# ScalarE scales the softmax rows, sums are kept in PSUM, four weight units get their own buffers, the last tile is finished in column halves

## The reference, cut to what matters

```python
branches = jnp.einsum('bsnc,ncd->bsnd', ys, w_branch)
gates = jax.nn.sigmoid(g.reshape(bn, s_len, N_BRANCH, D_MODEL).astype(jnp.float32))
merged = jnp.sum(gates * branches, axis=2)
return merged @ w_out
...
h = layer_norm(DEEPNORM_ALPHA * h + mix, ln1_g[l], ln1_b[l])
ffn = peer_ffn(h, peer_wq[l], peer_subkeys[l], peer_u[l], peer_v[l])
h = layer_norm(DEEPNORM_ALPHA * h + ffn, ln2_g[l], ln2_b[l])
```

## Time and profile before

| | |
|---|---|
| median of 3 runs | 1730.18 us (1727.88 to 1731.35) |
| the profiled execution | 1732.18 us, span 1730.4 us |
| granted TensorE clock, mean | 0.995 of full speed |
| PE busy | 1689.1 us (98%) |
| DVE, ACT, POOL busy | 1255.8, 768.7, 820.7 us |

### The profile page before, as it was taken

One profiled execution on the slowest core, in us unless ns is written; L12 is line 12 of the kernel. 1 busy time (PEld: TensorE's weight loads), 2 busy tenths in 40 slices (PEclk: granted clock), 3 DMA queues, 4 the chain that ended last, 5 costly groups with the idle time before them and its releaser, 6 DMA issues.

```text
span 1730.4 us, 24570 instructions
## 1 busy us (share of the span) xinstructions
PE 1689.1 (98%) x9061; PEld 1486.3 (86%) x9061; DVE 1255.8 (73%) x2490; ACT 768.7 (44%) x1301; POOL 820.7 (47%) x496
## 2 busy tenths in 40 slices
PE   7999999999999999999999999999999999999997
PEld 6667767778878999999999999999888888888886
DVE  2487896562353778789888987534888888888886
ACT  4444444522232443775577367534333333333332
POOL 5222222344446466766777677776433232332312
PEclk9999999999999999999999999999999999999998
DMA  5111111224233365899799789997999999999952
GB/s 200 61 62 50 59 60 54 77 94 146 84 112 110 113 197 186 306 372 345 253 333 384 249 286 386 383 364 296 405 390 354 384 376 351 383 372 354 389 190 85
DMA packets 126360, 417.65 MB, mean 241 GB/s; under 512 B 12961, under 2 KB 32417, under 8 KB 124705
## 3 DMA queue, kind: packets, MB, share of 16 engines
q1 hardware_dynamic: 70176, 232.81, 38.2%
q0 software_dynamic: 36864, 134.23, 20.6%
q10 hardware_dynamic: 19200, 49.03, 7.2%
HBM read 364.91 MB, written 50.86 MB: 240 GB/s over the span
## 4 chain that ended last, share of the span: by engine, by line
PE 88%; DVE 8%; ACT 2%; issue 1%; DMA 1%; POOL 0%; SPq 0%; another core or an unknown queue 0%; ACTq 0%; DVEq 0%; POOLq 0%
PE ps L1285 16%; PE ps L1287 16%; PE ps L1286 16%; PE ps L1514 11%; PE ps L1511 11%; PE ps L1512 11%; PE ps L1609 5%; PE ps L1370 1%; DVE dist_a L842 1%; DVE row L895 1%; DVE row L866 1%; DVE small L841 1%; PE ps L1395 1%; DVE small L892 1%; DMA raw<-w_units 0%
## 5 line engine op out<-in xcount | busy, mean ns | idle before, releaser
L1285 PE MATMUL ps<-tok_hi,w_hi 128*128 128x384 f32 (+2 forms) x1544 | 548.8, 355 | 8.4 <-issue 3.6
L1287 PE MATMUL ps<-tok_hi,w_lo 128*128 128x384 f32 (+2 forms) x1544 | 539.3, 349 | 0.0
L1286 PE MATMUL ps<-tok_lo,w_hi 128*128 128x384 f32 (+2 forms) x1544 | 539.3, 349 | 0.0
L539 ACT ACTIVATE w_hi<-raw 128x1024 fp32r<-128x1024 f32 x334 | 353.3, 1058 | 414.0 <-PE ps L1514 301.4
L486 POOL TENSOR_TENSOR w_lo<-raw,w_hi 128x1024 fp32r<-128x1024 f32 x128 | 318.2, 2489 | 165.8 <-ACT w_hi L539 165.2
L439 POOL TENSOR_TENSOR w_lo<-raw,w_hi 128x1024 fp32r<-128x1024 f32 x80 | 195.0, 2442 | 327.0 <-ACT w_hi L539 326.8
L1285 PEld LDWEIGHTS ps<-tok_hi,w_hi 128*128 128x128 f32 x1544 | 291.1, 189 | 35.7 <-issue 10.2
L1287 PEld LDWEIGHTS ps<-tok_hi,w_lo 128*128 128x128 f32 x1544 | 290.8, 188 | 18.6
L1286 PEld LDWEIGHTS ps<-tok_lo,w_hi 128*128 128x128 f32 x1544 | 291.3, 189 | 16.8
L1511 PE MATMUL ps<-w_hi,gh_hi 128*128 128x512 f32 x768 | 298.8, 389 | 0.0
L1512 PE MATMUL ps<-w_lo,gh_hi 128*128 128x512 f32 x768 | 298.8, 389 | 0.0
(11 more groups left out here) (208 smaller groups left out, 1866.9 us busy)
## 6 DMA issues: line engine op xcount, KB each, us to landing
raw<-u_units SPq DMA_DIRECT2D x128, 512.0 KB
raw<-v_rows SPq DMA_DIRECT2D x128, 512.0 KB
raw<-w_units SPq DMA_DIRECT2D x78, 512.0 KB
gate_d<-stage ACTq DMA_DIRECT2D x12, 2048.0 KB
gelu_d<-gelu_t ACTq DMA_DIRECT2D x120, 192.0 KB
gelu_in<-gelu_d SPq DMA_DIRECT2D x30, 768.0 KB
gate_in<-gate_d SPq DMA_DIRECT2D x28, 768.0 KB
gate_in<-gate_d SPq DMA_DIRECT2D x2, 1536.0 KB
```

Of the source, the lines that this page charges most:

```text
L539: act.activation(w_hi[:, n % RAW, :], raw[:, n % RAW, :], ACT.Copy).then_inc(hi_done, 1)
L1285: pe.matmul(out_, l_hi, r_hi, start=start, stop=False)
L1286: pe.matmul(out_, l_hi, r_lo, start=False, stop=False)
L1287: return pe.matmul(out_, l_lo, r_hi, start=False, stop=stop)
```

## The change

It has five parts.

1. In `exponents` ACT now waits for DVE's reciprocal (`rinv_set`) and does the two multiplications of the row itself (a copy with a scale); DVE's two are gone. This holds for the 24 items of C, B and A, not for D.
2. Merge: products and sums stay in PSUM banks where they can, and ACT makes `m_hi`. What PE waits for before it overwrites a bank changes with it: `m_set` for bank 3, for example.
3. First normalization: the sum, the subtraction of the mean and the product with `ln_g` are done by DVE in PSUM, the product with the inverse deviation and the sum with `ln_b` in one instruction into SBUF. POOL's part is gone. The first transposes stand one place earlier or later in PE's program.
4. The first four query units are split into `wq_hi` and `wq_lo` where the gates were, so these splits no longer wait for the slots of the output projection.
5. The last token tile of the second projection is computed in two column halves, each with its own sum and statistics; DVE finishes the tile in PSUM and stores it in two halves. ACT no longer normalizes that tile.

```diff
@@ ACT
                 if n >= RAW:
+                if U_WQ <= n < U_WQ + RAW:
+                    act.wait_ge(prod_set, 4 * KC)
+                elif U_WQ + RAW <= n < U_EXP:
+                    act.wait_ge(unit_done, n - 2 * RAW + 1)
...
                            act.activation(esink[:, ab, i:i + 1], sink_t[:, h:h + 1], ACT.Exp,
                                           bias=nbias[:, ab, i:i + 1]).then_inc(sink_exp, 1)
+                    act.wait_ge(rinv_set, soft_item(s) + 1)
+                    for ab in range(2):
+                        act.activation(row[s % 2][:, ab, :n], row[s % 2][:, ab, :n], ACT.Copy,
+                                       scale=rinv[:, ab, i:i + 1]).then_inc(probs_set, 1)
...
+            def merged_high(c):
+                act.wait_ge(merge_step, 3 * c + 3)
+                act.activation(m_hi[:, c, :], merged(c), ACT.Copy).then_inc(m_hi_set, 1)
@@ DVE
-                    link(dve.reciprocal(rinv[:, :, i], rsum[:, :, i]))
-                    for ab in range(2):
-                        dve.tensor_scalar(row[s % 2][:, ab, :n], row[s % 2][:, ab, :n], rinv[:, ab, i:i + 1],
-                                          None, ALU.mult).then_inc(probs_set, 1)
+                    dve.reciprocal(rinv[:, :, i], rsum[:, :, i]).then_inc(rinv_set, 1)
...
+            for c in range(KC):
+                if c >= NH:
+                    merged_low(c - 1)
+                gated(c, 0)
+                gated(c, 1)
+                if 0 < c < NH:
+                    merged_low(c - 1)
+                dve.wait_ge(prod_set, 4 * c + 2)
+                dve.tensor_tensor(branch_bank(c, 3), branch_bank(c, 3), prod[2][:], ALU.add).then_inc(merge_step, 1)
+                gated(c, 2)
+                gated(c, 3)
                 dve.wait_ge(prod_set, 4 * c + 4)
+                dve.tensor_tensor(prod[1][:], branch_bank(c, 0), prod[1][:], ALU.add).then_inc(merge_step, 1)
+                dve.wait_ge(merge_step, 3 * c + 2)
+                dve.tensor_tensor(merged(c), branch_bank(c, 3), prod[1][:], ALU.add).then_inc(merge_step, 1)
...
+            def norm_first(t, meanwhile=lambda: None):
+                one, z = slice(t, t + 1), ps[:, 2 * t:2 * t + 2, :].rearrange("p a n -> p (a n)")
...
+                link(dve.scalar_tensor_tensor(z, x_tok[:, t, :], ALPHA, z, ALU.mult, ALU.add))
...
+                dve.scalar_tensor_tensor(z, z, mean_var[:, t, 0:1], ln_g[:], ALU.subtract, ALU.mult).then_inc(norm1_set, 1)
+                meanwhile()
+                dve.wait_ge(std_set, t + 1)
+                newton_root(t)
+                dve.wait_ge(norm1_set, t + 1)
+                dve.scalar_tensor_tensor(x_tok[:, t, :], z, rstd[:, one], ln_b[:], ALU.mult, ALU.add).then_inc(h_set, 1)
@@ PE
-                    pe.wait_ge(prod_set, 4 * (c - (2 if c < NH else 1)) + (2, 3, 1, 0).index(b) + 1)
+                    before = c - (2 if c < NH else 1)
+                    if b == 3:
+                        pe.wait_ge(m_set, before + 1)
+                    elif b == 0:
+                        pe.wait_ge(merge_step, 3 * before + 2)
+                    else:
+                        pe.wait_ge(prod_set, 4 * before + (1 if b == 2 else 3))
...
-                       lambda t, k: transpose_h(k - 1) if (t, k) in ((3, 1), (3, 2)) else None)
+                       lambda t, k: transpose_h(t - 2) if (t, k) in ((2, 2), (3, 0)) else None)
...
+            last_halves(U_END - RAW, NT - 1, lambda k: (gh_hi[:, k, :], gh_lo[:, k, :]), NT - 2)
```

More of the change, by code:

```diff
@@ L322, in wait_lo, with hi_of, lo_of @@
                 engine.wait_ge(lo_dve, n - first - P + 1)
+    def hi_of(n):
+        return (wq_hi if U_WQ <= n < U_WQ + RAW else w_hi)[:, n % RAW, :]
+    def lo_of(n):
+        return (wq_lo if U_WQ <= n < U_WQ + RAW else w_lo)[:, n % RAW, :]
     def pair_slot(p):
@@ L417, in _ @@
                     sp.wait_ge(out_set, t + 1)
[L418 to L421, removed]
+                    sp.dma_start(out[t * P:(t + 1) * P, :], x_tok[:, t, :]).then_inc(out_done, 16)
+            for a in range(2):
+                cols = slice(S * a, S * a + S)
+                sp.wait_ge(last_set, a + 1)
+                sp.dma_start(out[(NT - 1) * P:NT * P, cols], x_tok[:, NT - 1, cols]).then_inc(out_done, 16)
+            sp.wait_ge(out_done, 16 * (NT + 1))
         @block.gpsimd
@@ L469, in _ @@
             for n in range(4, U_EXP + LO_AHEAD):
[L470 to L473, removed]
+                if n == U_WQ + RAW:
                     pool.wait_ge(sk_hi_set, 1)
@@ L655, in _ @@
                         .then_inc(sig_kept, 1)
+            merged_high(KC - 1)
             for n in range(U_OUT, U_WQ - HI_AHEAD):
@@ L795, in _ @@
                     finish_norm(0)
-            for t in range(1, NT):
+            for t in range(1, NT - 1):
                 finish_norm(t)
+            root(NT - 1, var2_set, std2_set)
         @block.vector
@@ L985, in norm, with newton_root @@
+            merged_low(KC - 1)
+            def newton_root(t):
+                one = slice(t, t + 1)
                 link(dve.reciprocal(rstd[:, one], stdev[:, one]))
@@ new lines, in norm_last @@
+            def norm_last():
+                t = NT - 1
+                one = slice(t, t + 1)
+                for a in range(2):
+                    cols, z = slice(S * a, S * a + S), ps[:, 2 * t + a, :]
+                    dve.wait_ge(last_full, a + 1)
+                    link(dve.scalar_tensor_tensor(z, x_tok[:, t, cols], ALPHA, z, ALU.mult, ALU.add))
+                    link(dve.bn_stats(stats[:, t, a], z))
+                link(dve.bn_aggr(mean_var[:, t], stats[:, t]))
+                dve.tensor_scalar(var_eps[:, one], mean_var[:, t, 1:2], EPS, None, ALU.add).then_inc(var2_set, 1)
+                z = ps[:, 2 * t:2 * t + 2, :].rearrange("p a n -> p (a n)")
+                dve.scalar_tensor_tensor(z, z, mean_var[:, t, 0:1], ln2_gt[:], ALU.subtract, ALU.mult).then_inc(last_times_g, 1)
+                dve.wait_ge(std2_set, t + 1)
+                newton_root(t)
+                dve.wait_ge(last_times_g, 1)
+                for a in range(2):
+                    cols = slice(S * a, S * a + S)
+                    dve.scalar_tensor_tensor(x_tok[:, t, cols], ps[:, 2 * t + a, :], rstd[:, one], ln2_bt[:, cols],
+                                             ALU.mult, ALU.add).then_inc(last_set, 1)
@@ L1273, in _ @@
             fmas_to(P)
-            for t in range(1, NT):
+            for t in range(1, NT - 1):
                 settle_tile(t)
-            dve.wait_ge(norm2_set, NT)
-            last_tile(ln2_gt, ln2_bt, last_set)
+            norm_last()
         @block.tensor
@@ L1515, in add_tile, with last_halves @@
                 return last
+            def last_halves(first, t, operands, column):
+                tile_ = slice(column * P, (column + 1) * P)
+                for a in range(2):
+                    o, cols = ps[:, 2 * t + a, :], slice(a * S, a * S + S)
+                    for k in range(RAW):
+                        s, (l_hi, l_lo) = (first + k) % RAW, operands(k)
+                        last = three(o, l_hi[:, tile_], l_lo[:, tile_], w_hi[:, s, cols], w_lo[:, s, cols],
+                                     False, k == RAW - 1)
+                    last.then_inc(last_full, 1)
             def last_units(first, tiles, ready, operands, full, between, before=0):
```

153 lines of the change are left out of this document (71 added, 82 removed).

## The result

The changed kernel takes 1737.68 us (median of 6 runs, 1736.77 to 1738.91) beside 1729.40 for the kernel before (6 runs): ratio 1.0048 (95% interval 1.0036 to 1.0060), 8.3 us slower. The forecast was 1739.2, 9.0 us slower. The profiled execution took 1736.77, its span is 1734.8.

A forecast was written before the change was run, and what follows sets the result against it. PE, busy 98% of the span, was taken to bound the kernel. The terms 18.4 - 3.9 - 3.2 - 2.3 = +9.0 us, against 1730.18, gave 1739.2 us; the range was 1729 to 1746.

The forecast's parts named there:

- its likeliest case: Whole kernel: slower, 1735 to 1743 us, chance 0.60.
- C, +8.6: Attention items of C: ACT waits for DVE's reciprocal, delaying copies PE needs; +8.6 us (6 to 9.8).
- B, -3.0: Attention items of B: eight PE pauses go, -4.2; A's first item meets POOL's low split, +1.2; -3.0 us.
- A's ring, +7.7: Attention turns 25 to 30: DVE and ACT steps form a loop that the scaling lengthens; +7.7 us, lower bound 5.
- Rival (b): Attention items of A: DVE or ACT has slack, so no loop delays PE; 1729.3 us, no change; chance 0.15.
- Clock, +5.1: Attention: PE's clock drops after three long pauses, 1.7 us each; +5.1 us (1.7 to 6.8).
- Rival (c): Attention: each item of C meets POOL's low split, the clock falls five times; +14 to +16, 1745 us; chance 0.15.
- Attention, +18.4: Attention loop in all: 8.6 - 3.0 + 7.7 + 5.1 = +18.4 us.
- Merge, -3.9: Merge: one new pause of 1.5, gate units start at 354.2 instead of 358.07; -3.9 us, -2 if the clock falls.
- First normalization, -3.2: First normalization: DVE sets the pace at 6.4 us a tile, one pause of 1.5 replaces 5.0; -3.2 us.
- the two sums that the prediction took as proof: DVE sums with PSUM input at 494.49 and 1719.20: both took 1.22 us, so such instructions aren't held by POOL.
- Tail, -2.3: Behind PE's last matmul: half sums start at once, DVE ends at 1724.9 instead of 1727.39; -2.3 us (-2.8 to -1.2).

The follow-up runs named there:

- the wait alone: Changed kernel with DVE scaling all rows, but ACT still waiting for the reciprocal in the C items: 1726.41 us, ratio 0.9983.
- part 1 alone: Kernel before with only the row scaling moved to ACT, merge, normalization and tail as before: 1752.39 us, ratio 1.0125.
- base: Changed kernel with DVE scaling all rows again, the other four parts kept: 1720.17 us, ratio 0.9938 to the kernel before.

## Why the prediction was right

Its time, 1739.2, is 1.5 from the measured one, and its likeliest case is the one that came. By its own steps:

- **C, +8.6.** Measured +7.6 in pauses: turn 5 5.41 - 0.78 = 4.6 (forecast 4.3, and 1.0 for an encounter with the low split, which came but held line 908 for 0.4 only); turn 6 3.47 - 0.79 = 2.7 (2.8); turns 0 to 3 1.30 - 0.34 - 0.70 = +0.3 (0.5). The pair's cost was 1.02 and 1.24 where 1.04 and 1.26 were taken. The kernel with the wait alone (4.41 and 2.13) shows the mechanism.
- **B, -3.0.** All eight waits of the earlier trace rows went, and A's first item waited 1.47 instead (DVE's line 908 took 1.95 there beside a low split): -2.7. Right in size, but "here the move helps" was half a truth: with B alone on ACT the encounter and the drop of the clock behind it cost the whole gain.
- **A's ring, +7.7.** The pauses forecast were 1.7, 0.3, 0.7, 2.0 and 3.5. The kernel with part 1 alone has 1.47, 0.22, 0.62, 1.89 and 3.54, less 0.52: +7.2. The changed kernel has 1.96 in the last place, for the reason above. Rival (b), no ring in A, falls with the kernel that scales A alone on ACT.
- **Clock, +5.1.** Five drops came where three were reckoned. One of them lies inside A's ring and costs nothing net, the other four 1.6 to 1.7 each: 6.6. The step that takes a pause as long as 2.33 to be followed by a drop, and a shorter one not, failed: drops followed pauses of 1.47 and 1.89, and none followed those of 2.36 and 2.34 in the two kernels with ACT's scaling and the old merge. Rival (c) had the five drops right, but its encounters weren't there in that size.
- **Attention, +18.4**: 7.6 - 2.7 + 7.2 + 6.6 = 18.7, the offsets say 18.8, the ratios of changed kernel and base 19.0 (1.0048 - 0.9938).
- **Merge, -3.9**: -3.7 in the trace, with the one pause of 1.5 that was forecast (1.41). The steps behind give some back; in the runs it is 3.1, with an interval about as wide, in the base and 6.9 in the changed kernel. That it is worth more in the changed kernel, where the clock stayed up behind the old merge's first pause, was not in the prediction.
- **First normalization, -3.2** (-3.6 to -2): mis-sized, it gave 4.6. DVE's tile took the 6.4 us forecast (505.81 to 512.18), but the one pause was 1.07, not 1.5, so 3.9 come from the pauses; another 0.7 isn't in the pauses and was not traced further. The term stands on two traces, since no run takes parts 3 and 4 back. The instructions in PSUM were not held: in the merge they took 0.69 and 0.70 beside a low split of 2.39, and DVE's whole first tile, with nothing over 1.28, ran beside four low splits (POOL's timeline):

```profile
504.10 9.48 POOL L455 TENSOR_TENSOR wq_lo<-raw,wq_hi 128x1024 fp32r<-128x1024 f32 x4
```

Of the two sums that the prediction took as proof, the one at 494.49 proves nothing, because POOL stood still beside it (from 492.56 to 499.57); beside the one at 1719.20 POOL ran from 1719.53 on. The Trainium skill ("SBUF — State Buffer", Who interferes with whom) lets only instructions that need the shared ports exclude each other; by that rule, the trace agrees.

- **Tail, -2.3** (-2.8 to -1.2): -1.7. DVE's end came 2.55 us nearer to the last matmul's end (5.7 instead of 8.2), and the store behind it takes 3.9 instead of 3.0, where "some tenths" had been set aside.

C was 1.0 too high and normalization 1.4 too small in the gain, the clock 1.5 too low: the errors nearly cancel, so the total is better than its terms, and that is luck. The comparison of two single traces would have misled by 3.7 us without the offsets, since the profiled execution before had two clock drops ahead of the loop that the one after lacks; the prediction had allowed 2.0 for that.

## What to carry to other kernels

Before work moves to a less busy engine, ask what stands behind the place in that engine's queue and who waits for it: ACT was 44% busy, yet 1.0 us of copying cost 4.6, because ACT then waited for DVE with another stage's copies behind it. A pause that comes from two engines excluding each other can be merely moved by moving one of them, as with all of B on ACT; look for what the held instruction will be next. With the last item left to DVE, 3.0 of the 4.2 us did go. And compare two traces by the offset of the same step, stage by stage, not by their ends.

## What the runs showed of the hardware that was not expected

PE makes the same pause of 2.51 us near 71 to 73 us in all 14 profiled executions (the change doesn't touch that place). In 8 of them the granted clock is about half of full speed in some stretch of the 3.4 us behind it, in 6 it stays at full. The kernel before:

```profile
73.10:76.40 3.30, 3.30 (x8) 2.63 (x9) 1.30 (x4) 0.34 (x1) 0.00 (x0) 0.50 0.00 0
```

and the changed kernel:

```profile
71.00:74.40 3.40, 3.40 (x17) 2.53 (x18) 1.29 (x4) 0.33 (x1) 0.00 (x0) 1.00 0.00 0
```

That is 1.7 us by chance, and two or three such places (3.4 to 5.1 us) are as much as most of the spread of a kernel's runs (2 to 8 us between the fastest and the slowest). The length of a pause alone doesn't decide: 1.47 was followed by a drop in the changed kernel and by none in the kernel with part 1 alone. What decides was not found out.

A DVE instruction on 128x2 numbers that met a low split on POOL ended with it, so its time goes by where in the split it begins: in the changed kernel 0.58 us when it began 1.81 us behind POOL's start (115.17), and 1.95 when it began 0.45 behind (269.51), against 0.17 alone. And a lower TensorE clock can make a stage shorter: the old merge reached its gates in 28.5 us in the two traces with a drop, and in 30.1 in the two without, with the same times on all engines up to the place where the clock fell or didn't.
